# Retiming the attention tasks of the first layer and splitting weight panels in halves

## The chip, the cores and the metric

The kernel runs on one core of one Trainium2 chip. Its time is the device time of one execution in microseconds (us), and the figure to compare is the median of several runs. PE is the matrix engine (TensorE), DVE the vector engine, ACT the scalar engine, POOL GpSimd, SP the engine that issues most DMAs. Each engine carries out its own instructions in order; semaphores tie them together.

## The reference

Four layers transform 256 latent tokens of width 1024. The two layers of the first block also carry 256 context tokens in the first of them. The change touches the mixer of layer 0, which adds two branches, and the treatment of the weights of all four layers.

```python
def mla_attend(q, k, v):            # branch 1: 8 heads, softmax attention
    s = einsum('bhqd,bhkd->bhqk', qblk, k) * scale
    p = softmax(s, axis=-1)
    return einsum('bhqk,bhkv->bhqv', p, v)
...
def gla_chunked(q, k, v, logg, s0): # branch 2: 4 heads, chunks of 64 tokens
    b = cumsum(logg.reshape(B, H, n, C, DK), axis=3)
    q_dec, k_inv, k_end = q * exp(b), k * exp(-b), k * exp(b[..., -1:, :] - b)
    a = where(incl, einsum('bhnid,bhnjd->bhnij', q_dec, k_inv), 0.0)
    o_intra = einsum('bhnij,bhnjv->bhniv', a, v)
    def step(s, xs):
        o = einsum('bhcd,bhdv->bhcv', qd_c, s)
        s = s * ge_c[..., None] + einsum('bhcd,bhcv->bhdv', ke_c, v_c)
        return s, o
```

Latent queries attend to all 512 keys, context queries to the 256 context keys. The recurrence (`gla_chunked`) runs forwards and backwards. Its output is normalised, gated, joined to the attention output and multiplied by `even_w_out`.

## The kernel before

**Weights.** All weights are stored as 204 panels, nearly all 128 x 2048 f32. SP streams them into three slots `raw`. ACT copies a panel to a rounded 32-bit form `w_high` (`split_act`, L355), DVE subtracts to get the remainder `w_low` (`split_dve`, L361), and PE then multiplies three times: low x high, high x high, high x low (`product3`, L389 to L391). `w_high` and `w_low` have two buffers each, so the copy of panel m waits until PE is done with panel m-2. PE waits for a panel's `w_low` before its first product.

**Attention tasks of layer 0.** There are 32 tasks (query tile i of 0 to 3, head h), all heads of tile 0 first. Tiles 0 and 1 are latent: 512 keys, a long task. Tiles 2 and 3 are context: 256 keys, a short task. Each task passes these stations: PE scores (L1399), DVE row maximum (`maxima`, L1525), ACT exponential (`exps`, L1476), PE transposes of the probabilities (`turn`, L1407), ACT copy out (`probs_out`, L1483), PE product with the values (`values`, L1418). PE's loop body is

```python
turn(n); scores(n + 2); gla_step(n); values(n)
```

ACT's is `exps(n); probs_out(n-1); gla_step(n)`, DVE's `maxima(n); gla_step(n)`. After 8 tasks of a tile DVE scales their sum (`scale`, L1531 and L1533).

**The recurrence among them.** `gla_step(n)` places pieces of the second branch at fixed task numbers on each engine: PE turns the keys (L1144), computes two groups of scores for each direction (L1159), which DVE masks (`mask_scores`, L1168), two groups of state updates (L1179), which DVE chains in seven steps (`gla_states`, L1188 and L1191), then outputs (L1207 and L1213), which ACT copies out (`outputs_out`, L1220 and L1221), sums of squares (L1228), roots on ACT (`roots`, L1233 and L1235, each with a table load) and gating on DVE (`gated`, L1240 and L1242). The gates of the backward direction are made in the first tasks (L1089 to L1138).

**Its end.** PE transposes the attention output (L1466), ACT and DVE split the eight blocks of features into high and low (L1516, L1519, L1566), and the product `even_out` starts (`linear`), taking blocks in the order that it is given.

Of the kernel before, what the change touches and what calls it, by code (L numbers as in the profile page):

```python
# [8 lines left out]
F32 = mybir.dt.float32  # L9
# [8 lines left out]
P = 128  # L18
# [268 lines left out]
class Program:  # L287
# [61 lines left out]
    def split_act(self, act, m, q=None):  # L349
        slot, width = m % RAW, PLAN[m]  # L350
        act.wait_ge(self.landed[slot], self.in_loop(self.landed_count, m, q))
        if m - 2 >= self.layer_m:
            sem = self.ends[m - 2][0]
            act.wait_ge(sem, self.in_loop(lambda x: self.ends[x][1], m - 2, q))
        self.nc.scalar.activation(self.wh[:, m % 2, 0:width], self.raw[:, slot, 0:width],  # L355
                                  ACT.Copy).then_inc(self.w_high, 1)

    def split_dve(self, dve, m, q=None):
        slot, width = m % RAW, PLAN[m]
        dve.wait_ge(self.w_high, self.in_loop(lambda x: x + 1, m, q))  # L360
        self.nc.vector.tensor_tensor(self.wl[:, m % 2, 0:width], self.raw[:, slot, 0:width],  # L361
                                     self.wh[:, m % 2, 0:width].bitcast(F32),
                                     ALU.subtract).then_inc(self.w_split, 1)

    def split_upto(self, which, eng, m):
        while self.split_next[which] <= m:
# [11 lines left out]
            self.split_upto("dve", dve, self.m + count - 1)  # L378

    def wait_split(self, pe, m, q=None):  # L380
        pe.wait_ge(self.w_split, self.in_loop(lambda x: x + 1, m, q))

    def product3(self, out, sh, sl, mh, ml, nk, opens=True, closes=True):

# [10 lines left out]
    def stream(self, end):  # L395

        total = min(end + RAW, len(PLAN))

        @self.block.sync
        def _(sp):  # L400
            n = self.streamed
            while n < RAW:
                sp.dma_start(self.raw[:, n, :], self.panels[n, :, :]).then_inc(self.landed[n], 16)
                n += 1
            turns = (total - n) // RAW
            with sp.Fori(0, turns) as q:
                for s in range(n, n + RAW):
                    sp.wait_ge(self.w_split, q * RAW + (s - RAW + 1))
                    sp.dma_start(self.raw[:, s % RAW, :],
                                 self.panels[ds(q * RAW + s, 1), :, :].rearrange("a p n -> p (a n)")  # L410
                                 ).then_inc(self.landed[s % RAW], 16)
            for n in range(n + turns * RAW, total):
                sp.wait_ge(self.w_split, n - RAW + 1)
# [604 lines left out]
def even_mixer(pr, mod, scope, norm_w, x_ready, beside, rest):  # L1018
# [346 lines left out]
    def beside_uv(which, eng, p):  # L1365
        if which == "dve":
# [27 lines left out]
    def _(pe):  # L1394
# [16 lines left out]
        def values(n):  # L1411
            i, h = tasks[n]
            keys = width(n) // P
            pe.wait_ge(t_out, n + 1)
            if h == 0 and i >= 2:
                pe.wait_ge(a_scaled, i - 1)
            for j in range(keys):
                last = nc.tensor.matmul(ps[:, 4 + i % 2, h * MV:(h + 1) * MV], prob_t[:, n % 2, j * P:(j + 1) * P],  # L1418
                                        v[:, first_key(i) // P + j, h * MV:(h + 1) * MV],
                                        start=(j == 0), stop=(j == keys - 1))  # L1420
            last.then_inc(v_done, 1)

        def gla_step(n):
            if n == 2:
# [4 lines left out]
            if n in (7, 8):  # L1429
                gla_updates(pe, 0, n - 7)  # L1430
            if n == 9:
                pe.wait_ge(s_ready[0], 2)
                turn_keys(pe, 1)
            if n in (10, 11):
                gla_scores(pe, 1, n - 10)
            if n in (13, 14):
                gla_updates(pe, 1, n - 13)
            if n in (16, 17):
                gla_outputs(pe, 0, (0, 1) if n == 16 else (2, 3))
            if n in (19, 20):  # L1440
                gla_outputs(pe, 1, (0, 1) if n == 19 else (2, 3))
            if n in (22, 24):
                square_sums(pe, (n - 22) // 2)

        pe.wait_ge(z_taken[0], 1)
        gate_products(pe, 1)
# [13 lines left out]
        for i in range(4):  # L1460
            pe.wait_ge(a_scaled, i + 1)
            if i == 0:
                pe.wait_ge(p_ready, T)
                pe.wait_ge(t_out, T)
            for b in range(4):
                last = nc.tensor.transpose(ps[:, b, i * P:(i + 1) * P], att[:, i, b * P:(b + 1) * P], c("ident"))  # L1466
                if i == 3:
                    last.then_inc(a_turned, 1)

    @pr.block.scalar  # L1470
    def _(act):
# [12 lines left out]
                .then_inc(t_out, 1)  # L1484

        def gla_step(n):
            if n == 1:
                gate_abs(act, 1)
            if n == 2:
                gate_log(act, 1)  # L1490
            if n == 3:
                keys_out(act, 0)
            if n == 4:
                decays_first(act, 1)
            if n == 5:
                decays_second(act, 1)
            if n == 10:
                keys_out(act, 1)
            if n in (18, 21):
                outputs_out(act, (n - 18) // 3)  # L1500
            if n in (22, 24):
                act.wait_ge(o_done, 2)
                pr.split_upto("act", act, pr.m + (n - 22) // 2)
            if n in (23, 25):
                roots(act, (n - 23) // 2)

        for n in range(T + 1):
            if n < T:
# [2 lines left out]
                probs_out(n - 1)  # L1511
            gla_step(n)
        act.wait_ge(s_done, T)
        for k in range(4):
            act.wait_ge(o_gated, k // 2 + 1)
            nc.scalar.activation(high[:, 4 + k, :], gla[:, k, :], ACT.Copy).then_inc(y_high, 1)  # L1516
        for b in range(4):
            act.wait_ge(a_turned, b + 1)
            nc.scalar.activation(high[:, b, :], ps[:, b, :], ACT.Copy).then_inc(y_high, 1)  # L1519

    @pr.block.vector
    def _(dve):
# [3 lines left out]
                .then_inc(m_ready, 1)  # L1526

        def scale(i):
            group = slice(i * H, (i + 1) * H)
            dve.wait_ge(p_ready, (i + 1) * H)  # L1530
            ch.then(dve, nc.vector.reciprocal(inv[:, group], total[:, group]))  # L1531
            dve.wait_ge(v_done, (i + 1) * H)
            nc.vector.tensor_tensor(att[:, i, :].rearrange("p (h n) -> p h n", n=MV),  # L1533
                                    ps[:, 4 + i % 2, :].rearrange("p (h n) -> p h n", n=MV),
                                    spread(inv[:, group], 2, MV), ALU.mult).then_inc(a_scaled, 1)

        def gla_step(n):
            if n == 1:
                gate_min(dve, 1)
            if n == 3:  # L1540
                gate_sums(dve, 1)
            if n in (4, 5):
                mask_scores(dve, 0, n - 4)
            if n == 6:
                decayed(dve, 1)
            if n in (7, 8):
                gla_states(dve, 0, n - 7)
            if n in (10, 11):
                mask_scores(dve, 1, n - 10)
            if n in (13, 14):  # L1550
                gla_states(dve, 1, n - 13)
            if n in (23, 25):
                pr.split_upto("dve", dve, pr.m + (n - 23) // 2)
            if n in (24, 26):
                gated(dve, (n - 24) // 2)

        for n in range(T):
            maxima(n)
            gla_step(n)
            if n >= H and (n - 1) % H == 0:  # L1560
                scale(n // H - 1)
        scale(3)
        for k in range(8):
            dve.wait_ge(y_high, k + 1)
            src = gla[:, k, :] if k < 4 else ps[:, k - 4, :]
            nc.vector.tensor_tensor(low[:, (k + 4) % 8, :], src, high[:, (k + 4) % 8, :].bitcast(F32),  # L1566
                                    ALU.subtract).then_inc(y_split, 1)

    return high, low, [(y_split, KD)], later

# [1260 lines left out]
def build(nc, panels, rows, conditions, small, xin, pos, out):  # L2831
    with ExitStack() as ctx:
# [41 lines left out]
        def layer0():  # L2874
# [6 lines left out]
            def _(sp):  # L2881
# [17 lines left out]
            ready = pr.linear("even_out", 4, 2, 8, pr.features(high, low, TA, KD, tall_offset, [4, 5, 6, 7, 0, 1, 2, 3]),  # L2899
                              pr.add_gated(mod, 16, 2, TA), y_split, engines=("dve",), banks=(4, 5, 6, 7),  # L2900
                              after=gates_ready, rising=True,
                              beside=lambda which, eng, p: take_rest(eng, 2) if which == "dve" else None)
# [120 lines left out]
```

## Time and profile before

| | |
|---|---|
| median of 3 runs | 2465.21 us (2463.22 to 2465.62) |
| profiled execution | 2460.01 us, span 2458.2 us |
| PE busy | 2077.2 us (85%), mean granted clock 0.920 |
| DVE busy | 1528.6 us (62%) |
| ACT busy | 869.9 us (35%) |
| attention stage, first scores to the first product of `even_out` | 221.44 to 393.83 us |

Busy time counts compute instructions; the granted clock is a share of TensorE's full speed. In the rows below a time in front is the start within the span, the next the duration; "x8" is that many instructions merged; a bracket says how long the engine was idle before and what ended that. The trace counts every 32-bit matmul of L1159, L1179, L1399 and L1418 as two instructions. In the tables of windows a stretch is followed by the busy time of each engine and by the granted clock under PEclk.

### The profile page before, as it was taken

The numbers are of one execution on the slowest core, as the hardware profiler recorded it, in microseconds if no ns is written. First come the engines' busy times: TensorE is split into PE (matmuls) and PEld (weight loads), VectorE is DVE, ScalarE is ACT, GpSimd is POOL, SyncE is SP. The second block draws the span as 40 slices with busy tenths as digits, with TensorE's granted clock in tenths as the row PEclk, the third lists the DMA queues.
The fourth block names the chain that finished last, engine by engine and source line by source line (L and its number), as shares of the span: only waits on it lengthen the run. The fifth ranks groups of instructions, "written<-read, shape, count | busy, mean of one in ns | idle before, by whom it ended". The sixth has DMA issues, their size and how long they took to land. (4 is left out here: it accounts for less than half of the span.)

```text
span 2458.2 us, 39406 instructions
## 1 busy us (share of the span) xinstructions
PE 2077.2 (85%) x16738; PEld 1843.5 (75%) x16738; DVE 1528.6 (62%) x2187; ACT 869.9 (35%) x1104; POOL 140.3 (6%) x231
## 2 busy tenths in 40 slices
PE   0898679799999588769996999699789979978997
PEld 0686467577888476568886899688679978867997
DVE  7865326699777556655654666668466656845444
ACT  2335233322222222142224444345443334534442
POOL 0000000000110001010210000000000000000000
PEclk9999688899999779879998999889899988979999
DMA  7432002355553245300001477433147733313552
GB/s 303 153 136 69 1 16 88 111 176 179 201 192 140 99 159 184 119 2 3 3 3 56 169 262 265 173 120 123 67 145 267 266 144 137 121 52 105 186 188 86
DMA packets 59018, 323.89 MB, mean 132 GB/s; under 512 B 6272, under 2 KB 7424, under 8 KB 32512
## 3 DMA queue, kind: packets, MB, share of 16 engines
q1 hardware_dynamic: 32960, 227.91, 26.1%
q0 software_dynamic: 25344, 92.29, 10.6%
q8 instruction: 105, 1.72, 0.3%
q10 hardware_dynamic: 576, 1.70, 0.2%
q14 instruction: 33, 0.27, 0.0%
HBM read 320.83 MB, written 1.05 MB: 131 GB/s over the span
## 5 line engine op out<-in xcount | busy, mean ns | idle before, releaser
L361 DVE TENSOR_TENSOR w_low<-raw,w_high 128x2048 fp32r<-128x2048 f32 (+1 forms) x204 | 458.9, 2252 | 323.6 <-ACT w_high L355 323.4
L355 ACT ACTIVATE w_high<-raw 128x2048 fp32r<-128x2048 f32 (+1 forms) x204 | 382.8, 1878 | 427.9 <-PE banks L391 382.2
L498 DVE SCALAR_TENSOR_TENSOR mod_rows<-mod_rows,silu_condition 128x1024 f32<-128x1024 f32 x176 | 212.4, 1221 | 48.2 <-DMA mod_rows<-rows_dram 46.6
L389 PE MATMUL banks<-ffn_a_l,w_high 128*128 128x256 f32 x704 | 201.0, 285 | 5.5 <-DVE ffn_hidden L860 5.5
L390 PE MATMUL banks<-ffn_a_h,w_high 128*128 128x256 f32 x704 | 199.4, 283 | 0.0
L391 PE MATMUL banks<-ffn_a_h,w_low 128*128 128x256 f32 x704 | 199.3, 283 | 0.0
L389 PE MATMUL banks<-mlp_a_l,w_high 128*128 128x512 f32 (+1 forms) x512 | 177.9, 347 | 17.8 <-DVE mlp_hidden L862 10.0
L484 POOL DMA_DIRECT2D mod_rows<-rows_dram x176 | 93.1, 529 | 1542.8 <-DVE mod_rows L498 1389.2
L389 PE MATMUL banks<-mlp_hidden_l,w_high 128*128 128x512 f32 (+1 forms) x512 | 173.7, 339 | 3.1 <-DVE mlp_hidden_l L868 2.1
L391 PE MATMUL banks<-mlp_a_h,w_low 128*128 128x512 f32 (+1 forms) x512 | 175.2, 342 | 0.0
L390 PE MATMUL banks<-mlp_a_h,w_high 128*128 128x512 f32 (+1 forms) x512 | 175.2, 342 | 0.0
L390 PE MATMUL banks<-mlp_hidden_h,w_high 128*128 128x512 f32 (+1 forms) x512 | 173.0, 338 | 0.0
L391 PE MATMUL banks<-mlp_hidden_h,w_low 128*128 128x512 f32 (+1 forms) x512 | 173.0, 338 | 0.0
L389 PEld LDWEIGHTS banks<-ffn_a_l,w_high 128*128 128x128 f32 x704 | 133.9, 190 | 10.7 <-issue 5.9
L389 PE MATMUL banks<-mix_l,w_high 128*128 128x256 f32 x432 | 127.6, 295 | 11.8 <-DVE mix_l L631 7.9
L390 PEld LDWEIGHTS banks<-ffn_a_h,w_high 128*128 128x128 f32 x704 | 133.9, 190 | 0.0
L391 PEld LDWEIGHTS banks<-ffn_a_h,w_low 128*128 128x128 f32 x704 | 133.8, 190 | 0.0
L389 PEld LDWEIGHTS banks<-mlp_a_l,w_high 128*128 128x128 f32 x512 | 97.9, 191 | 36.8 <-issue 14.4
L390 PE MATMUL banks<-mix_h,w_high 128*128 128x256 f32 x432 | 123.8, 287 | 0.0
L391 PE MATMUL banks<-mix_h,w_low 128*128 128x256 f32 x432 | 123.5, 286 | 0.0
L389 PEld LDWEIGHTS banks<-mlp_hidden_l,w_high 128*128 128x128 f32 x512 | 96.4, 188 | 16.4 <-DVE mlp_y L880 3.2
L391 PEld LDWEIGHTS banks<-mlp_a_h,w_low 128*128 128x128 f32 x512 | 97.9, 191 | 11.7
(582 smaller groups left out, 4930.9 us busy)
## 6 DMA issues: line engine op xcount, KB each, us to landing
raw<-panels_dram SPq DMA_DIRECT2D x204, 1024.0 KB, 4.8
mod_rows<-rows_dram POOLq DMA_DIRECT2D x176, 512.0 KB, 5.0
mod_0a_rows<-rows_dram SPq DMA_DIRECT2D x4, 2048.0 KB, 24.9
x_features<-x_features_dram SPq DMA_DIRECT2D x1, 2048.0 KB, 25.2
constants<-small_dram SPq DMA_DIRECT2D x1, 1660.5 KB, 16.3
silu_condition<-conditions_dram ACTq DMA_DIRECT2D x3, 512.0 KB, 5.9
out_dram<-x_features SPq DMA_DIRECT2D x1, 1024.0 KB, 4.8
constants<-small_dram SPq DMA_DIRECT2D x1, 736.5 KB, 5.5
```

The source lines that it names most:

```text
L355: self.nc.scalar.activation(self.wh[:, m % 2, 0:width], self.raw[:, slot, 0:width], ACT.Copy).then_inc(self.w_high, 1)
L361: self.nc.vector.tensor_tensor(self.wl[:, m % 2, 0:width], self.raw[:, slot, 0:width], self.wh[:, m % 2, 0:width].bitcast(F32), ALU.subtra ...
L389: self.nc.tensor.matmul(out, sh(k), ml(k), start=(opens and k == 0), stop=False)
L390: self.nc.tensor.matmul(out, sh(k), mh(k), start=False, stop=False)
L391: last = self.nc.tensor.matmul(out, sl(k), mh(k), start=False, stop=(closes and k == nk - 1))
L484: pool.dma_start(buffers[i % nb], self.rows[at, :, :]).then_inc(landed[i % nb], 16)
L498: nc.vector.scalar_tensor_tensor(row if v == nv - 1 else self.scratch[:], row, 1.0, self.cond[v][:], ALU.mult, ALU.mult, accum_out=mod[:, ...
```

## The change

1. Every panel is split in two halves by columns: two ACT copies, two DVE subtractions, each DVE half waiting for its ACT half; PE still waits for both.
2. Tasks of a long and a short tile alternate (tiles 0 and 2, then 1 and 3), and PE issues `turn(n+1)` and `scores(n+3)` ahead of `gla_step(n)` and `values(n)`.
3. The pieces of the recurrence sit at other task numbers; DVE and ACT take what PE made for them two or three task numbers later than before.
4. `scale` and the final splitting follow the new order; `gated` moves from inside the loop to behind it, and `even_out` takes blocks in the order 4, 5, 0, 1, 2, 3, 6, 7.

```diff
-        self.nc.scalar.activation(self.wh[:, m % 2, 0:width], self.raw[:, slot, 0:width],
-                                  ACT.Copy).then_inc(self.w_high, 1)
+        for h in range(2):
+            cols = slice(h * width // 2, (h + 1) * width // 2)
+            self.nc.scalar.activation(self.wh[:, m % 2, cols], self.raw[:, slot, cols],
+                                      ACT.Copy).then_inc(self.w_high, 1)
...
+        for h in range(2):
+            cols = slice(h * width // 2, (h + 1) * width // 2)
+            dve.wait_ge(self.w_high, self.in_loop(lambda x: 2 * x + h + 1, m, q))
+            self.nc.vector.tensor_tensor(self.wl[:, m % 2, cols], ...).then_inc(self.w_split, 1)
...
-    tasks = [(i, h) for i in range(4) for h in range(H)]
+    tasks = [(i, h) for first in range(2) for h in range(H) for i in (first, first + 2)]
...
+        turn(0)
+        scores(2)
         for n in range(T):
-            turn(n)
-            if n + 2 < T:
-                scores(n + 2)
+            if n + 1 < T:
+                turn(n + 1)
+            if n + 3 < T:
+                scores(n + 3)
             gla_step(n)
             values(n)
...
-            if n in (4, 5):                       # PE
-                gla_scores(pe, 0, n - 4)
+            if n in (3, 5):
+                gla_scores(pe, 0, (n - 3) // 2)
...
-            if n in (4, 5):                       # DVE
-                mask_scores(dve, 0, n - 4)
+            if n in (6, 8):
+                mask_scores(dve, 0, (n - 6) // 2)
...
-            if n in (22, 24):                     # ACT
+            if n in (28, 30):
                 act.wait_ge(o_done, 2)
-                pr.split_upto("act", act, pr.m + (n - 22) // 2)
+                pr.split_upto("act", act, pr.m + (n - 28) // 2)
-            if n in (23, 25):
-                roots(act, (n - 23) // 2)
+            if n in (29, 31):
+                roots(act, (n - 29) // 2)
...
-        scale(3)
+        gated(dve, 0)
+        scale(1)
+        scale(3)
+        gated(dve, 1)
```

On PE, around the first scores of the recurrence (L1159, in the changed file L1163), before the change; L1407 are the turned probabilities, L1399 the scores, L1418 the values:

```order
L1407 MATMUL banks<-constants,even_pa 128x128 x4
L1399 MATMUL banks<-mla_k,mla_q 128x512
L1159 MATMUL banks<-even_y 128x128 x8
L1418 MATMUL banks<-mla_v,mla_prob_t 128x64 x4
L1407 MATMUL banks<-constants,even_pa 128x128 x4
L1399 MATMUL banks<-mla_k,mla_q 128x512
L1159 MATMUL banks<-even_y 128x128 x8
```

The same place on PE in the changed kernel, where these three lines are L1411, L1403 and L1422:

```order
L1411 MATMUL banks<-constants,even_pa 128x128 x4
L1403 MATMUL banks<-mla_k,mla_q 128x512
L1163 MATMUL banks<-even_y 128x128 x8
L1422 MATMUL banks<-mla_v,mla_prob_t 128x64 x2
L1411 MATMUL banks<-constants,even_pa 128x128 x2
L1403 MATMUL banks<-mla_k,mla_q 128x256
L1422 MATMUL banks<-mla_v,mla_prob_t 128x64 x4
L1411 MATMUL banks<-constants,even_pa 128x128 x4
L1403 MATMUL banks<-mla_k,mla_q 128x512
L1163 MATMUL banks<-even_y 128x128 x8
```

The two groups of scores now have a task without a piece between them, and a row of L1411 turns the task after the one whose values follow it.

On DVE the maxima (L1525) and the masking (L1168) of the forward direction before the change:

```order
L1525 TENSOR_REDUCE mla_stat<-banks 128x1
L1168 COPY_PREDICATED gla_att<-constants,banks 128x1024
L1525 TENSOR_REDUCE mla_stat<-banks 128x1
L1168 COPY_PREDICATED gla_att<-constants,banks 128x1024
L1525 TENSOR_REDUCE mla_stat<-banks 128x1
```

The same place on DVE in the changed kernel (L1533 and L1172), with the three products of `decayed` (L1139 to L1142) now in between:

```order
L1533 TENSOR_REDUCE mla_stat<-banks 128x1 x3
L1172 COPY_PREDICATED gla_att<-constants,banks 128x1024
L1533 TENSOR_REDUCE mla_stat<-banks 128x1
L1139 TENSOR_TENSOR gla_work_230<-even_pb,gla_work_230 128x1024
L1140 SCALAR_TENSOR_TENSOR gla_work_231<-even_pb,gla_work_231 128x1024
L1142 TENSOR_TENSOR gla_work_231<-even_pb,gla_work_231 128x1024
L1533 TENSOR_REDUCE mla_stat<-banks 128x1
L1172 COPY_PREDICATED gla_att<-constants,banks 128x1024
```

Three maxima stand ahead of the first masking where one stood, so the maxima of the tasks whose scores PE has issued are out before DVE waits for the recurrence.

On ACT the last tasks of the changed kernel (L1483 exponential, L1490 copy out, L357 panel halves, L1237 and L1239 roots):

```order
L357 ACTIVATE w_high<-raw 128x1024 x2
L1483 ACTIVATE even_pa,mla_stat<-banks,mla_stat 128x256
L1490 ACTIVATE mla_prob_t<-banks 128x512
L1237 ACT_TABLE_LOAD
L1237 ACTIVATE even_y<-banks,constants 128x1024
L1239 ACT_TABLE_LOAD
L1239 ACTIVATE even_y<-even_y 128x1024
L1490 ACTIVATE mla_prob_t<-banks 128x256
L1524 ACTIVATE even_h<-even_pa 128x512 x2
```

The second root now stands directly ahead of the last task's copy out; before, six tasks stood between them.

## Rows read from the trace of the kernel before

**Rows 1.** Windows: the attention stage, and two stretches of it.

```profile
221.40:394.00 172.60, 123.28 (x746) 95.17 (x746) 56.71 (x92) 64.17 (x128) 2.80 (x4) 0.75 0.06 19
326.60:337.00 10.40, 10.39 (x55) 9.37 (x56) 1.65 (x4) 2.52 (x8) 0.00 (x0) 0.56 0.01 2
337.00:361.00 24.00, 20.96 (x192) 18.56 (x190) 2.12 (x5) 7.76 (x18) 0.00 (x0) 0.93 0.00 1
```

**Rows 2.** Waits in the attention stage: engine, line, releaser, total us, times, longest.

```profile
PE banks L1418 <- ACT mla_prob_t L1483: 48.6, 17, 4.6
```

**Rows 3.** Timeline of one long task with its recurrence piece.

```profile
286.36 1.88 PE L1144 MATMUL banks<-constants,gla_work 128*128 128x128 f32 x8
288.07 1.01 PE L1418 MATMUL banks<-mla_v,mla_prob_t 128*128 128x64 f32 x8
...
290.31 1.16 PE L1159 MATMUL banks<-gla_work 64*128 64x128 f32 x16
291.59 1.29 DVE L1168 COPY_PREDICATED gla_att<-constants,banks 128x1024 f32<-128x1024 uint32 x1 [9.48 <-PE banks L1159]
...
293.49 0.69 ACT L1476 ACTIVATE even_pa<-banks,mla_stat 128x512 f32<-128x512 f32 x1 [4.19 <-DVE mla_stat L1525]
...
294.80 1.91 PE L1418 MATMUL banks<-mla_v,mla_prob_t 128*128 128x64 f32 x8 [3.33 <-ACT mla_prob_t L1483]
```

**Rows 4.** Timeline of PE: half of an output piece, a short task, sums of squares.

```profile
354.05 1.08 PEld L1207 LDWEIGHTS banks<-gla_att,even_gv 128*128 128x128 f32 x8
...
357.96 0.66 PE L1418 MATMUL banks<-mla_v,mla_prob_t 128*128 128x64 f32 x4
...
360.80 0.66 PE L1418 MATMUL banks<-mla_v,mla_prob_t 128*128 128x64 f32 x4 [1.52 <-ACT mla_prob_t L1483]
...
361.95 1.88 PE L1228 MATMUL banks<-even_y,constants 128*128 128x512 f32 x4
```

**Rows 5.** Timeline: one group of state updates at full clock.

```profile
265.33 1.10 PE L1179 MATMUL banks<-even_gv,even_y 64*64 64x128 f32 x28
```

**Rows 6.** Timeline of DVE: the gate sums' start, and the maximum behind them.

```profile
233.37 1.23 DVE L1109 TENSOR_TENSOR gla_work<-gla_work,gla_work 128x1024 f32<-128x1024 f32 x1 [4.12 <-ACT gla_work L1104]
...
239.40 0.68 DVE L1525 TENSOR_REDUCE mla_stat<-banks 128x1 f32<-128x512 f32 x1
```

**Rows 7.** Timeline of ACT: an output copied out, and one root with table loads.

```profile
344.45 1.02 ACT L1221 ACTIVATE even_y<-banks 128x1024 f32<-128x1024 f32 x1
...
363.29 1.28 ACT L1233 ACT_TABLE_LOAD   x1
...
367.97 0.46 ACT L1476 ACTIVATE even_pa<-banks,mla_stat 128x256 f32<-128x256 f32 x1
```

**Rows 8.** Timeline of the stage's end: last copy out, first product of `even_out`.

```profile
389.59 0.38 ACT L1483 ACTIVATE mla_prob_t<-banks 128x256 f32<-128x256 f32 x1 [0.97 <-PE banks L1407]
...
393.83 0.50 PE L389 MATMUL banks<-even_l,w_high 128*128 128x512 f32 x1
```

**Rows 9.** The page's costliest groups: busy, mean ns, idle before and releaser.

```profile
L361 DVE TENSOR_TENSOR w_low<-raw,w_high 128x2048 fp32r<-128x2048 f32 (+1 forms) x204 | 458.9, 2252 | 323.6 <-ACT w_high L355 323.4
L355 ACT ACTIVATE w_high<-raw 128x2048 fp32r<-128x2048 f32 (+1 forms) x204 | 382.8, 1878 | 427.9 <-PE banks L391 382.2
```

**Rows 10.** Waits of PE in the whole kernel behind panels and hidden activations.

```profile
PE banks L389 <- DVE w_low L361: 11.0, 6, 3.0
PE banks L389 <- DVE mlp_hidden L862: 10.0, 16, 2.5
...
PE banks L389 <- DVE ffn_hidden L860: 5.5, 11, 0.9
```

**Rows 11.** Timeline of a feed-forward turn in layer 1: panel, modulation row, hidden activation.

```profile
1475.22 2.29 DVE L361 TENSOR_TENSOR w_low<-raw,w_high 128x2048 fp32r<-128x2048 f32 x1 [1.98 <-ACT w_high L355]
...
1478.57 0.69 DVE L862 SCALAR_TENSOR_TENSOR mlp_hidden<-banks,mlp_activated 128x512 f32<-128x512 f32 x1
```

**Rows 12.** Timeline: DVE operations of 1024 columns, back to back.

```profile
205.16 1.22 DVE L1136 SCALAR_TENSOR_TENSOR even_y<-even_pb,even_y 128x1024 f32<-128x1024 f32 x1
206.30 1.22 DVE L1138 TENSOR_TENSOR even_y<-even_pb,even_y 128x1024 f32<-128x1024 f32 x1
```

More of the change, by code:

```diff
@@ L1414, in values @@
             pe.wait_ge(t_out, n + 1)
-            if h == 0 and i >= 2:
-                pe.wait_ge(a_scaled, i - 1)
+            if h == 0 and i % 2:
+                pe.wait_ge(a_scaled, i // 2 + 1)
             for j in range(keys):
-                last = nc.tensor.matmul(ps[:, 4 + i % 2, h * MV:(h + 1) * MV], prob_t[:, n % 2, j * P:(j + 1) * P],
+                last = nc.tensor.matmul(ps[:, 4 + i // 2, h * MV:(h + 1) * MV], prob_t[:, n % 2, j * P:(j + 1) * P],
                                         v[:, first_key(i) // P + j, h * MV:(h + 1) * MV],
@@ L1453, in _ @@
         scores(1)
+        turn(0)
+        scores(2)
         for n in range(T):
-            turn(n)
-            if n + 2 < T:
-                scores(n + 2)
+            if n + 1 < T:
+                turn(n + 1)
+            if n + 3 < T:
+                scores(n + 3)
             gla_step(n)
             values(n)
-        for i in range(4):
-            pe.wait_ge(a_scaled, i + 1)
+        for n, i in enumerate((0, 2, 1, 3)):
+            pe.wait_ge(a_scaled, n + 1)
             if i == 0:
@@ L1513, in _ @@
         act.wait_ge(s_done, T)
[L1514 to L1519, printed above, removed]
+        for k in (4, 5, 0, 1, 2, 3, 6, 7):
+            if k >= 4:
+                act.wait_ge(o_gated, k // 2 - 1)
+                nc.scalar.activation(high[:, k, :], gla[:, k - 4, :], ACT.Copy).then_inc(y_high, 1)
+            else:
+                act.wait_ge(a_turned, k + 1)
+                nc.scalar.activation(high[:, k, :], ps[:, k, :], ACT.Copy).then_inc(y_high, 1)
     @pr.block.vector
@@ L1541, in gla_step @@
                 gate_sums(dve, 1)
-            if n in (4, 5):
-                mask_scores(dve, 0, n - 4)
-            if n == 6:
+            if n in (6, 8):
+                mask_scores(dve, 0, (n - 6) // 2)
+            if n == 7:
                 decayed(dve, 1)
[L1546 to L1555, printed above, removed]
+            if n in (10, 12):
+                gla_states(dve, 0, (n - 10) // 2)
+            if n in (16, 18):
+                mask_scores(dve, 1, (n - 16) // 2)
+            if n in (20, 22):
+                gla_states(dve, 1, (n - 20) // 2)
+            if n in (29, 31):
+                pr.split_upto("dve", dve, pr.m + (n - 29) // 2)
         for n in range(T):
@@ L1559, in _ @@
             gla_step(n)
-            if n >= H and (n - 1) % H == 0:
-                scale(n // H - 1)
-        scale(3)
[L1563 to L1567, printed above, removed]
+            if n == 17:
+                scale(0)
+            if n == 18:
+                scale(2)
+        gated(dve, 0)
+        scale(1)
+        scale(3)
+        gated(dve, 1)
+        for n, k in enumerate((4, 5, 0, 1, 2, 3, 6, 7)):
+            dve.wait_ge(y_high, n + 1)
+            nc.vector.tensor_tensor(low[:, k, :], gla[:, k - 4, :] if k >= 4 else ps[:, k, :],
+                                    high[:, k, :].bitcast(F32), ALU.subtract).then_inc(y_split, 1)
     return high, low, [(y_split, KD)], later
@@ L2898, in layer0 @@
                 pr, mod, ab, norm("norm1", 0), mod_ready + [(x_in, 16)], beside, rows_rest)
-            ready = pr.linear("even_out", 4, 2, 8, pr.features(high, low, TA, KD, tall_offset, [4, 5, 6, 7, 0, 1, 2, 3]),
+            ready = pr.linear("even_out", 4, 2, 8, pr.features(high, low, TA, KD, tall_offset, [4, 5, 0, 1, 2, 3, 6, 7]),
                               pr.add_gated(mod, 16, 2, TA), y_split, engines=("dve",), banks=(4, 5, 6, 7),
```

64 lines of the change are left out of this document (32 added, 32 removed).

## The prediction

> **What bounds the kernel now.** I read the page first, then the windows by stage, the waits, and the timeline of the stage that the change rewrites. The windows show the attention stage of layer 0 taking 172.6 us, with PE busy 123.28 us at a mean granted clock of 0.75 [rows 1]. The waits name the cause: PE stood 48.6 us in 17 places ahead of the values L1418 until ACT had copied out the probabilities [rows 2]. The timeline shows why. PE issues scores of the recurrence L1159 at 290.31; DVE takes them at 291.59, having waited 9.48 us in its own order; only then come the maximum and at 293.49 ACT's exponential of the next task, and ACT's order has the copy out of this task behind that exponential; so the values of this task wait 3.33 us, to 294.80 [rows 3]. Four maskings and four chains of states repeat this circle. It has a second price: the same eight instructions of L1418 took 1.01 us at 288.07 and 1.91 us at 294.80 [rows 3]. The second runs after PE stood still, at half the clock.
>
> In the rest of the kernel PE is mostly the bound. Each weight panel goes ACT 1878 ns, then DVE 2252 ns, and DVE stood 323.4 us in total waiting for ACT in this [rows 9]. That matters only where PE waits behind it.
>
> **The attention stage, part by part.** The new order breaks the circle. PE issues `scores(n+3)`, so the maximum of task n+2 or n+3 is out before DVE waits for the recurrence piece of task n. ACT copies task n's probabilities out while PE turns n+1. So I add up what PE itself must do, at full clock, from the starts of following rows. A long task: values at 288.07 to the piece at 290.31, 2.24 us [rows 3]. A short one: 360.80 to 361.95, 1.15 us [rows 4]. Sixteen of each: 54.2 us. Recurrence: turned keys 286.36 to 288.07 at half clock, so 0.86, twice, 1.7; scores 1.16 x 4 = 4.6 [rows 3]; updates 1.10 x 4 = 4.4 [rows 5]; output halves 354.05 to 357.96, 3.91 x 4 = 15.6; squares 1.88 x 2 = 3.8 [rows 4]. In all 84.3 us, where the stage before took 393.83 - 221.44 = 172.4 us.
>
> PE isn't the bound to the end. ACT's last pieces hang on the last output half. Behind that half PE has only the squares (3.8) and the rest of five tasks (about 4.6 tasks of 1.7, 7.9 us), so it ends 84.3 - 11.7 = 72.6 us of PE work in. ACT then has, in its order: copying the output out, two of 1.02, 2.0 us [rows 7]; two panels of 1.88, 3.8 us [rows 9]; two roots with two table loads each, 363.29 to 367.97, 4.68 x 2 = 9.4 us [rows 7]; and exponentials and copies of four and a half tasks at about 1 us each (the exponential alone is 0.69 at 293.49 [rows 3]), 4.5 us. Together 19.7 us, more than PE's 11.7. The last copy out, which now stands behind the second root, comes there. From it to `even_out` there were 393.83 - 389.59 = 4.2 us [rows 8]. The changed DVE order puts `gated(1)`, two operations of 1.22 us [rows 12], ahead of the splitting of the first block: 0 to 2.4 us more, I take 1.2, since fewer transposes are left by then. 5.4 us.
>
> Stalls that stay: at the start the first exponential must come before the first turn, 1.4 us; ACT's log of the backward gates has the pattern of a root, 4.7 us [rows 7], and the third exponential now stands behind it, 4.5 us; the gate sums hold DVE from 233.37 to the maximum at 239.40, 6 us [rows 6], of which about 1.5 us stick out over the slack of two tasks; the three products of `decayed`, 3 x 1.22 us [rows 12] ahead of a maximum, 2 us. Together 9.4 us.
>
> Sum at full clock: 72.6 + 19.7 + 5.4 + 9.4 = 107.1 us. Two allowances. After each of these early stalls the clock falls, as in [rows 3], and work of about 10 us runs at half: 10 us. Handovers that the sum passes over, a few tenths in some places of thirty: 6 us. The stage comes to about 124 us, **48 us less**. Bounds: neither allowance, 107, 65 less; all PE work up to the last output half at half clock, below.
>
> **The clock** is the weak point. PE was busy 10.39 of 10.40 us from 326.6 on and had only 0.56 of full clock; from 337 to 361, in the same mixture, it had 0.93 with 20.96 of 24 us busy [rows 1]. So continuous work takes a while to be granted full clock, and keeps it over short gaps. The Trainium skill, "TensorE: Matmul & The Clock Gate", Part 1, says that the throttled clock is the default and activity releases it, and under HAM oscillation that a kernel with repeated idle gaps starts each burst cold. By that rule a stage whose stalls go gets the full clock for nearly all its work, the upper bound of the gain; the slow first row above says that the trace agrees only with delay.
>
> **The halves.** Per panel one more ACT and one more DVE instruction. DVE: two of 1.22 us against 2.25, at most 0.19 more [rows 9, 12]; back to back they start 1.14 us apart (205.16, 206.30), so at least 0.03 [rows 12]. ACT: two of 1.02 (a copy of 1024 columns [rows 7]) against 1.88, at most 0.16. Panel to ready goes from 1.88 + 2.25 = 4.13 us to 1.02 + 2.3 = 3.3: 0.8 us sooner wherever DVE stands waiting. The feed-forward turn shows it: DVE waited 1.98 us for ACT, subtracted for 2.29 us, made a modulation row, and came to the hidden activation at 1478.57, for which PE then waited [rows 11]. Those PE waits are 10.0 us in 16 places and 5.5 us in 11, and 6 on panels themselves, 11.0 us [rows 10]. Mean waits of 0.5 to 0.6 us lie below the 0.8 us gained, so about 12 us of the 15.5 go, and 6 x 0.8 = 4.8 of the 11.0: 17 us. Against that, DVE or ACT lie on the path between products, at norms and in the mixers, where up to a fifth of the 204 panels may be: 40 x 0.13 = 5 us. Net **12 us less**; bounds 17 less and, with 71 us (204 x 0.35) wholly on the path and no gain, 71 more.
>
> The Trainium skill, "VectorE: DVE Perf Modes", section on the TRN2 errata, says that VectorE and ScalarE pay a fixed extra per instruction on SBUF sources and asks for large tiles, which speaks against the halves. "Perfetto Trace Analysis", Optimizing Scalar/DVE Operations, puts about 60 ns (VectorE) and 93 ns (ScalarE) on each; by it 204 panels cost 31 us of engine time, an estimate from that page, little of it on the path. [Rows 12] agree with a small fixed cost. It also allows breaking up instructions where they leave bubbles on other engines.
>
> **Sum.** 2460.0 (profiled execution) - 48 - 12 = 2400. That execution lay 5.2 us under the median, so against the median 2465.2 - 60 = **2405 us**. What a measurement of this kernel can tell from no change is about 0.2%, 5 us.
>
> **Rivals.**
> - *Everything overlaps and the clock stays full* (chance 0.12). 65 less in the stage, 17 in the halves: 2465 - 82 = 2383. For it: [rows 1] from 337 on. Against it: the early stalls are in the order itself.
> - *Stalls move instead of going* (0.17). DVE's chains of states or ACT's wait for an output hold the next maximum or exponential after all, because tasks are now only 1.7 us long on average, less than the 2.24 us of today's long ones, so two tasks of slack are 3.4 us. If half of the 48.6 us [rows 2] stays, the stage gains 24 us: 2465 - 24 - 12 = 2429.
> - *Half clock throughout* (0.09). If the stage never earns full clock, 72.6 us becomes 72.6 x 1.9 = 138 (1.91 against 1.01 us [rows 3]) and the stage 138 + 19.7 + 5.4 + 9.4 = 172.5, as before. Only the halves count: 2453. For it: the first window of [rows 1]; this is what the skill's rule makes of a loop whose matmuls stay too sparse.
> - *The change doesn't do what it says* (0.06). The tail on ACT or another order lengthens the stage by what the loop saves and the halves give about what they cost: 2455 to 2470.
> - *Slower* (0.04). The second half's instruction lies on the path of nearly every panel, because DVE's order, not PE, paces the layers: 204 x 0.35 = 71 us more, 48 less from attention: 2488. It decides from 0.24 us per panel (48/204) on. Against it: DVE waited for ACT at these panels for 323.4 us [rows 9], so it has time.
>
> **Numbers.** My forecast has 0.52, with a range of its own of 2390 to 2422. With the cases on both sides, 2387 to 2445 leaves out part of the first rival, the half clock and the slower cases. Faster by over 0.2%: 0.52 + 0.12 + 0.17 + 0.09 = 0.90; within 0.2%: 0.05; slower: 0.05.
>
> **What would show it.** The stage from the first scores to the first product of `even_out` should last 115 to 130 us, with a clock of 0.85 or more. PE's wait ahead of the values should fall from 48.6 to under 12 us. ACT should be busy nearly without gaps in the last 20 us, PE idle there. The waits of PE for `mlp_hidden` and `ffn_hidden` should fall from 15.5 to about 4 us. ACT's and DVE's halves should be near 1.0 and 1.2 us, 408 of each. I am wrong if the clock stays near 0.75 with PE busy throughout, if DVE's chains of states still end long waits of ACT's exponential, or if the layers after the first get longer.

## The result

The changed kernel takes 2366.82 us (median of 4 runs, 2366.02 to 2374.3), the kernel before 2464.22 us in the same comparison (4 runs). The ratio is 0.9614, 95% interval 0.9591 to 0.9638: 97 us less. The direction was forecast, the size wasn't: 2405 us with a range from 2387 was 38 us too slow, and even the rival in which everything goes well (2383 us) was.

The profiled execution has a span of 2365.3 us against 2458.2, so 92.9 us less. The time between the same two places in each kernel:

| stretch | before, us | after, us | less |
|---|---|---|---|
| first scores to first product of `even_out` | 172.4 | 107.8 | 64.6 |
| feed-forward of layer 0, first to last hidden activation | 330.2 | 327.7 | 2.5 |
| feed-forward of layer 1, the same | 181.5 | 171.1 | 10.3 |
| feed-forward of layer 2, the same | 176.4 | 169.7 | 6.8 |
| feed-forward of layer 3, the same | 170.5 | 169.7 | 0.8 |
| all the rest (mixers, norms) | | | 7.9 |

**The attention stage.** The windows of the changed kernel, first the whole stage, then a part near its start, its middle and its end; the columns are those of [rows 1]:

```profile
221.37:329.14 107.77, 93.47 (x745) 73.87 (x745) 55.52 (x92) 63.94 (x130) 2.76 (x4) 0.92 0.09 30
231.60:238.00 6.40, 6.40 (x35) 5.18 (x36) 5.02 (x6) 3.57 (x10) 0.00 (x0) 0.73 0.01 3
238.00:305.00 67.00, 65.45 (x611) 53.18 (x611) 31.76 (x62) 30.92 (x77) 0.00 (x0) 0.97 0.01 1
305.00:329.14 24.14, 16.82 (x80) 12.60 (x79) 13.36 (x17) 21.08 (x32) 0.00 (x0) 0.79 0.25 87
```

From 238 to 305 us PE is busy 65.45 of 67 us at a granted clock of 0.97. The whole stage has 0.92 where [rows 1] had 0.75. PE's two largest sums of waits in it:

```profile
PE banks L1411 <- ACT even_pa L1483: 11.0, 5, 4.2
PE banks L1422 <- ACT mla_prob_t L1490: 2.2, 1, 2.2
```

The 48.6 us ahead of the values of [rows 2] are down to 2.2. In their place stand 11.0 us ahead of the turn, three at the start (1.16, 4.18 and 1.55 us) and two at the end (0.62 and 3.45 us). The timeline shows the first masking of the recurrence, the piece that held everything up in [rows 3]; L1163 is PE's piece, L1422 the values, L1411 the next turn:

```profile
238.88 1.16 PE L1163 MATMUL banks<-even_y 64*128 64x128 f32 x16
...
239.97 0.66 PE L1422 MATMUL banks<-mla_v,mla_prob_t 128*128 128x64 f32 x4
240.16 1.31 DVE L1172 COPY_PREDICATED gla_att<-constants,banks 128x1024 f32<-128x1024 uint32 x1 [0.48 <-PE banks L1163]
...
240.47 0.39 PE L1411 MATMUL banks<-constants,even_pa 128*128 128x128 f32 x2
```

PE goes from its piece to the values and on to the next turn without a bracket, that is without having been idle, and DVE masks beside it. The start and the tail:

```profile
231.59 0.95 PE L1411 MATMUL banks<-constants,even_pa 128*128 128x128 f32 x4 [4.18 <-ACT even_pa L1483]
...
304.43 1.02 ACT L1224 ACTIVATE even_pa<-banks 128x1024 f32<-128x1024 f32 x1 [3.88 <-PE banks L1217]
...
323.61 0.36 ACT L1490 ACTIVATE mla_prob_t<-banks 128x256 f32<-128x256 f32 x1
...
329.14 0.47 PE L393 MATMUL banks<-even_l,w_high 128*128 128x512 f32 x1 [1.10 <-DVE even_l L1577]
```

**The halves.** The page's groups of the changed kernel, to be set against [rows 9]:

```profile
L365 DVE TENSOR_TENSOR w_low<-raw,w_high 128x1024 fp32r<-128x1024 f32 (+1 forms) x408 | 472.8, 1201 | 268.4 <-ACT w_high L357 268.1
L357 ACT ACTIVATE w_high<-raw 128x1024 fp32r<-128x1024 f32 (+1 forms) x408 | 401.8, 1034 | 434.0 <-PE banks L395 388.5
```

DVE's busy time rose by 13.9 us, 68 ns for each of 204 added instructions, ACT's by 19.0 us, 93 ns each. The Trainium skill, "Perfetto Trace Analysis", Optimizing Scalar/DVE Operations, gives about 60 and 93 ns; ACT's figure here is the same, DVE's is 8 ns higher.

PE's waits behind panels and hidden activations in the whole kernel, where [rows 10] had 11.0, 10.0 and 5.5 us:

```profile
PE banks L393 <- DVE w_low L365: 9.3, 5, 3.2
...
PE banks L393 <- DVE mlp_hidden L866: 4.0, 2, 2.5
...
PE banks L393 <- DVE ffn_hidden L864: 1.9, 2, 0.9
```

Two successive hidden activations of layer 1's feed-forward in the changed kernel:

```profile
1402.96 0.69 DVE L866 SCALAR_TENSOR_TENSOR mlp_hidden<-banks,mlp_activated 128x512 f32<-128x512 f32 x1
...
1414.35 0.69 DVE L866 SCALAR_TENSOR_TENSOR mlp_hidden<-banks,mlp_activated 128x512 f32<-128x512 f32 x1
```

and the one that followed the row at 1478.57 of [rows 11] in the kernel before:

```profile
1490.62 0.69 DVE L862 SCALAR_TENSOR_TENSOR mlp_hidden<-banks,mlp_activated 128x512 f32<-128x512 f32 x1
```

A turn took 12.05 us and takes 11.39. This is what PE did before the change at the wait behind that row at 1478.57:

```profile
1478.53 0.28 PE L390 MATMUL banks<-mlp_hidden_h,w_high 128*128 128x256 f32 x1
1478.64 0.28 PE L391 MATMUL banks<-mlp_hidden_h,w_low 128*128 128x256 f32 x1
1479.31 0.39 PE L389 MATMUL banks<-mlp_a_l,w_high 128*128 128x256 f32 x1 [0.39 <-DVE mlp_hidden L862]
1479.53 0.29 PE L390 MATMUL banks<-mlp_a_h,w_high 128*128 128x256 f32 x1
```

In an unbroken row the products start 0.12 us apart. Here 0.67 us pass from one start to the next and then 0.22, so the row loses 0.65 us, though the bracket counts 0.39 of idle: it counts from the modelled end of the last product, 1478.92, and in an unbroken row each product overlaps the next. The lost 0.65 us are nearly the whole 0.66 by which the turn shrank.

### The profile page after: what moved, and what is told of

It is laid out like the page before. It is cut to its first block and busy times, and to the rows that moved or that the text cites. A ratio compares the mean times of both kernels' runs of the same rounds, so it can differ in the third digit from the quotient of the medians.

```text
span 2365.3 us, 39903 instructions
## 1 busy us (share of the span) xinstructions
PE 2036.8 (86%) x16738; PEld 1818.3 (77%) x16738; DVE 1540.9 (65%) x2391; ACT 888.1 (38%) x1308; POOL 140.3 (6%) x231
## 5 line engine op out<-in xcount | busy, mean ns | idle before, releaser
L365 DVE TENSOR_TENSOR w_low<-raw,w_high 128x1024 fp32r<-128x1024 f32 (+1 forms) x408 | 472.8, 1201 | 268.4 <-ACT w_high L357 268.1
L357 ACT ACTIVATE w_high<-raw 128x1024 fp32r<-128x1024 f32 (+1 forms) x408 | 401.8, 1034 | 434.0 <-PE banks L395 388.5
L394 PEld LDWEIGHTS banks<-mlp_a_h,w_high 128*128 128x128 f32 x512 | 98.0, 192 | 10.9
## 6 DMA issues: line engine op xcount, KB each, us to landing
constants<-small_dram SPq DMA_DIRECT2D x1, 1660.5 KB, 16.3
```

The costliest lines, as they stand in the source:

```text
L357: self.nc.scalar.activation(self.wh[:, m % 2, cols], self.raw[:, slot, cols], ACT.Copy).then_inc(self.w_high, 1)
L365: self.nc.vector.tensor_tensor(self.wl[:, m % 2, cols], self.raw[:, slot, cols], self.wh[:, m % 2, cols].bitcast(F32), ALU.subtract).then_ ...
L394: self.nc.tensor.matmul(out, sh(k), mh(k), start=False, stop=False)
```

## The experiments

Ratios are to runs of the kernel before on the same chip. "Stage" is the stretch in the first line of the table above.

**1. The halves alone.** The kernel before with the edits to `split_act`, `split_dve`, `wait_split` and `stream`, nothing else.

```diff
+        for h in range(2):
+            cols = slice(h * width // 2, (h + 1) * width // 2)
...
+            dve.wait_ge(self.w_high, self.in_loop(lambda x: 2 * x + h + 1, m, q))
```

> The kernel before with the panel halves alone. Theory A (the two parts are independent; the layers behind layer 0 shrank by 28 us through the halves alone): attention stage 172 us as before, whole kernel about 2436 us, feed-forward turns 11.4 us in layer 1 and 17.1 us in layer 2 (12.06 and 17.7 before). Rival B (the later layers gained from an earlier start of modulation rows and DMA, not from the halves): the turns keep 12.06 and 17.7 us and the kernel stays at 2455 to 2470 us.

Measured 2434.48 us against 2461.18, ratio 0.988 (0.9859 to 0.99): 26.7 us less. The stage doesn't shrink: it has 176.8 us in the profiled execution, 4.4 more than before, at the same mean clock of 0.75. That execution was the slowest of the four, 7.6 us above their median, so whether the halves lengthen this stage is not shown. The feed-forward stretches are those of the changed kernel within 1.4 us: 329.0, 171.1, 169.7 and 169.7 us. PE's waits for hidden activations are too:

```profile
PE banks L393 <- DVE mlp_hidden L866: 4.0, 2, 2.5
PE banks L393 <- DVE ffn_hidden L864: 1.9, 2, 0.9
```

Theory A holds, rival B falls: the later layers gain through the halves, whatever attention does.

**2. The attention order alone.** The changed kernel with whole panels.

```diff
-        for h in range(2):
-            cols = slice(h * width // 2, (h + 1) * width // 2)
+        self.nc.scalar.activation(self.wh[:, m % 2, 0:width], self.raw[:, slot, 0:width], ...)
```

> The changed kernel with whole panels. Theory A: attention stage about 108 us with its clock at 0.92, the rest as before, whole kernel about 2400 us. Rival B: about 2370 us, since the later layers shrink here too. Rival C (the halves also shorten the tail of the stage by letting DVE start sooner): stage 112 us or more.

Measured 2394.5 us, ratio 0.9724 (0.9704 to 0.9743): 66.7 us less. The window of the stage:

```profile
220.89:327.27 106.38, 92.28 (x746) 73.48 (x745) 55.32 (x90) 63.56 (x128) 2.77 (x4) 0.92 0.09 31
```

106.4 us, 1.4 us less than with halves, so rival C falls, and rival B with it. The two gains add up: 26.7 + 66.7 = 93.4 of 97.4 us, and 0.988 x 0.9724 = 0.9607 beside the measured 0.9614.

**3. Without alternation.** Run-ahead, late taking and halves kept, the tasks tile by tile.

```diff
-    tasks = [(i, h) for first in range(2) for h in range(H) for i in (first, first + 2)]
+    tasks = [(i, h) for i in range(4) for h in range(H)]
...
+            if n in (10, 18, 26):
+                scale((n - 10) // 8)
```

> The changed kernel with the tasks in their old order, all heads of a tile before the next tile: run-ahead, later taking and halves stay. Long tasks come first, all short ones last, beside the output pieces and ACT's roots. Theory A (alternation is a minor part: the PE work is the same sum): stage 108 to 114 us, whole kernel 2367 to 2373 us. Rival D (alternation carries the gain, because short tasks alone are shorter than ACT's and DVE's pieces, and four of them don't cover a root): stage above 120 us, kernel above 2380 us.

Measured 2368.88 us, ratio 0.9616 (0.9597 to 0.9636). The window of the stage:

```profile
220.47:328.94 108.47, 92.86 (x745) 73.85 (x745) 55.70 (x92) 63.42 (x130) 2.76 (x4) 0.92 0.09 30
```

108.5 against 107.8 us. Rival D falls. With run-ahead and late taking in place, alternating long and short tasks brings nothing here that can be measured; without them it was not tried.

**4. Without run-ahead.** PE's old loop body with the new task numbers.

```diff
-        turn(0)
-        scores(2)
         for n in range(T):
-            if n + 1 < T:
-                turn(n + 1)
-            if n + 3 < T:
-                scores(n + 3)
+            turn(n)
+            if n + 2 < T:
+                scores(n + 2)
...
-                eng.wait_ge(o_out, 1)
+                eng.wait_ge(o_squared, 1)
```

> The changed kernel with PE's old loop body (turn n, scores n+2, piece, values n); the later taking, alternation and halves stay; the second output piece also waits for the squares of the first. Theory E (the later taking breaks the circle, run-ahead only hides ACT's copy out): the waits ahead of the values come back at every task for the copy out, 0.5 to 1 us in 32 places, stage 125 to 140 us, kernel about 2390 us. Rival F (without run-ahead the values of task n wait for the exponential of n+1, which waits for DVE just as before): stage near 165 us, kernel about 2430 us.

Measured 2383.85 us, ratio 0.9685 (0.9663 to 0.9706). Window and longest waits of PE in the stage:

```profile
220.93:341.98 121.05, 96.64 (x745) 73.67 (x745) 54.94 (x92) 64.36 (x131) 2.77 (x4) 0.92 0.08 27
...
PE banks L1422 <- ACT mla_prob_t L1487: 10.3, 5, 3.7
PE banks L1183 <- DVE gla_att L1172: 2.8, 2, 2.4
PE banks L1211 <- DVE gla_work L1195: 1.8, 1, 1.8
```

Rival F falls. The stage has 121.1 us, below theory E's 125 to 140: ahead of the values there are 10.3 us in 5 places, not a wait at each of 32. New are waits of PE for DVE's results of the recurrence. So run-ahead is worth 13 us of the 64.6 by the stage in the profiled executions, and 17 us by the medians of the whole kernel.

**5. Taken early.** Run-ahead stays, but DVE takes PE's pieces one task number behind PE instead of three.

```diff
-            if n in (6, 8):
-                mask_scores(dve, 0, (n - 6) // 2)
+            if n in (4, 6):
+                mask_scores(dve, 0, (n - 4) // 2)
...
-            if n in (10, 12):
-                gla_states(dve, 0, (n - 10) // 2)
+            if n in (8, 10):
+                gla_states(dve, 0, (n - 8) // 2)
```

> The changed kernel, but DVE masks the scores and chains the states one task number behind PE's piece instead of three (run-ahead, alternation, ACT's places and halves stay). Theory E (taking later is what breaks the circle): DVE waits for PE's piece with a maximum behind it that PE soon needs, eight times 1 to 3 us, stage 120 to 130 us, kernel 2380 to 2390 us, clock in the stage below 0.9. Rival G (run-ahead alone gives enough slack): stage 108 to 112 us, kernel within 5 us of the changed one (2367).

Measured 2405.72 us, ratio 0.9769 (0.9748 to 0.979). Window, PE's waits, and one chain of states in the timeline (L1183 PE's updates, L1192 and L1195 DVE's chain, L1483 the exponential):

```profile
220.91:359.64 138.73, 103.34 (x745) 80.85 (x745) 54.81 (x92) 62.59 (x130) 2.76 (x4) 0.87 0.07 24
...
PE banks L1411 <- ACT even_pa L1483: 28.4, 13, 4.2
...
256.04 1.98 PE L1183 MATMUL banks<-even_gv,even_y 64*64 64x128 f32 x28
...
258.06 0.29 DVE L1192 COPY even_y<-banks 128x128 f32<-128x128 f32 x1 [5.64 <-PE banks L1183]
258.39 2.27 DVE L1195 SCALAR_TENSOR_TENSOR even_y<-even_y,gla_g_end,banks 128x128 f32<-128x128 f32 x6
...
261.02 0.47 ACT L1483 ACTIVATE even_pa<-banks,mla_stat 128x256 f32<-128x256 f32 x1 [7.51 <-DVE mla_stat L1533]
...
261.64 0.63 PE L1411 MATMUL banks<-constants,even_pa 128*128 128x128 f32 x2 [2.86 <-ACT even_pa L1483]
```

DVE stood 5.64 us at the chain with the next maximum behind it, ACT waited 7.51 us for that maximum, PE 2.86 us for the exponential. Rival G falls. Theory E was right about the mechanism but not about the size: it forecast 120 to 130 us for the stage, which has 138.7, and 2380 to 2390 for the kernel, which has 2405.7. Late taking is worth 31 us by the stage, more than run-ahead. The profiled execution was 7 us faster than the median; by the medians of the whole kernel it is 39 us. Updates at half clock (1.98 us here, 1.10 in [rows 5]) are part of that.

**6. Rows later, whole panels.** The new attention order and whole panels. In the feed-forwards of layers 1 to 3 DVE makes its modulation rows behind the hidden activation (layer 3 has none to make).

```diff
                 split(which, m_of["down", cs, 0], q)(eng)
-                rows(eng, 1)
+                if not keep:
+                    rows(eng, 1)
                 if keep:
                     split(which, m_of["down", cs, 0] + 1, q)(eng)
-                    rows(eng, 2)
...
                 high_or_low(eng, cs + 1, q)
+                if keep:
+                    rows(eng, 1)
+                    rows(eng, 2)
```

> New attention order, whole panels, and in the feed-forwards with kept sums DVE makes its modulation rows behind the hidden activation's low part instead of ahead of the hidden activation. Theory H (PE waited because panel, subtraction and row stand ahead of the hidden activation in DVE's order; anything that takes 0.7 us out of that sum gives back 0.7 us a turn): turns of 11.4 us in layer 1 and 17.1 us in layer 2 as with the halves, kernel about 2383 us (17 of the halves' 28 us). Rival I (the halves gain by making panels ready for PE sooner, not through the hidden activation): turns stay at 12.06 and 17.7 us, kernel about 2400 us.

Measured 2378.36 us, ratio 0.9654 (0.9634 to 0.9675), 16 us less than experiment 2. Rival I falls. DVE in two successive turns of layer 1:

```profile
1408.48 0.68 DVE L862 SCALAR_TENSOR_TENSOR mlp_hidden<-banks,mlp_activated 128x512 f32<-128x512 f32 x1
...
1410.47 1.22 DVE L498 SCALAR_TENSOR_TENSOR mod_rows<-mod_rows,silu_condition 128x1024 f32<-128x1024 f32 x1
...
1419.88 0.68 DVE L862 SCALAR_TENSOR_TENSOR mlp_hidden<-banks,mlp_activated 128x512 f32<-128x512 f32 x1
```

The turn is 11.40 us with whole panels; that of layer 2 is 17.1 us. So the waits there came from the sum of what stood ahead of the hidden activation in DVE's order, and the halves are one way to shorten it. The fall of layer 1's stretch is 11.0 us and of layer 2's 6.0, within 1 us of the halves' 10.3 and 6.8.

**7. Quarters.**

```diff
-        for h in range(2):
-            cols = slice(h * width // 2, (h + 1) * width // 2)
+        for h in range(4):
+            cols = slice(h * width // 4, (h + 1) * width // 4)
```

> The changed kernel with panels in four quarters: 408 more instructions on ACT and on DVE. Theory H: a panel is ready at 0.55 + 4 x 0.6 = about 3.0 us instead of 3.4 us, but PE no longer waits in the feed-forward turns, so nothing is left to win there; the fixed cost (0.03 to 0.06 us per piece) is paid in the mixers and at norms: kernel 2366 to 2376 us. Rival J (readiness of panels still bounds the layers): 2355 to 2362 us.

Measured 2373.0 us, ratio 0.9635 (0.9615 to 0.9656), so rival J falls; 6 us above the changed kernel's 2366.8 and 4 above its repetition in experiment 9. The intervals of the ratios overlap, so a loss is not shown; there is no gain. The page:

```profile
L365 DVE TENSOR_TENSOR w_low<-raw,w_high 128x512 fp32r<-128x512 f32 (+1 forms) x816 | 500.5, 676 | 238.9 <-ACT w_high L357 236.9
L357 ACT ACTIVATE w_high<-raw 128x512 fp32r<-128x512 f32 (+1 forms) x816 | 440.0, 612 | 424.1 <-PE banks L395 377.0
```

408 more instructions each cost 27.7 us of DVE and 38.2 us of ACT, 68 and 94 ns apiece, as the first halving did. The feed-forward stretches of layers 1 to 3 hardly moved (170.7, 169.4 and 169.4 us).

**8. Joined roots.** ACT takes both roots in one go, with two table loads fewer, and both gatings come ahead of the last scaling.

```diff
-            if n in (29, 31):
-                roots(act, (n - 29) // 2)
+            if n == 29:
+                root_log(act, 0)
+                pr.split_upto("act", act, pr.m + 1)
+                root_log(act, 1)
+                root_exp(act, 0)
+                root_exp(act, 1)
```

> The changed kernel with ACT's two roots joined: logarithm 0, second panel, logarithm 1, then both exponentials, so two table loads fewer; both gatings ahead of the last scaling; blocks in the order 4, 5, 6, 7, 0, 1, 2, 3. Theory K (ACT's order bounds the last 23 us of the stage): two loads of 1.28 us and the 1.1 us wait of the first product go, stage 3 to 4.5 us shorter, kernel about 2363 us. Rival L (PE's order bounds the end): no change, 2367 us.

Measured 2368.73 us, ratio 0.9617 (0.9595 to 0.9638). Both expectations failed in part. The stage did shrink, to 105.9 us, and the last product of `even_out` started 2.1 us sooner (371.5 against 373.6 us), but nothing reached the end. Most of it is lost at the next norm, where PE sums squares. First the changed kernel, its timeline and a window:

```profile
376.66 7.13 PE L555 MATMUL banks<-norm_squares,constants 128*128 128x512 f32 x16 [2.67 <-ACT norm_squares L542]
...
376.00:383.00 7.00, 6.34 (x15) 2.96 (x16) 5.91 (x19) 5.53 (x10) 1.28 (x3) 1.00 0.93 355
```

Then the kernel with joined roots:

```profile
374.62 8.83 PE L555 MATMUL banks<-norm_squares,constants 128*128 128x512 f32 x16 [2.67 <-ACT norm_squares L542]
...
376.00:383.00 7.00, 7.00 (x15) 2.85 (x13) 3.90 (x15) 3.49 (x6) 0.00 (x0) 0.84 0.95 393
```

The same sixteen instructions, behind the same wait of 2.67 us, took 1.70 us longer at a clock of 0.84 instead of 1.00. It isn't the earlier arrival alone that does this: in experiment 3 the sixteen started at 376.49 and also took 8.83 us, in the kernel of experiment 10 they started at 375.96 and took 7.13. What decides it is not shown.

**9 to 11. The same, together.** The changed kernel once more, then it with the later rows, then it with later rows and joined roots, five rounds on one chip.

> The changed kernel itself, on the chip that runs the next two: about 2367 us, stage 108 us.

> The changed kernel, halves kept, with DVE's modulation rows of the kept feed-forwards behind the hidden activation. Theory H (halves and later rows remove the same wait of PE): nothing is left to gain in the turns, 11.4 and 17.0 us as in the changed kernel, kernel within 2 us of it. Rival I (they act in different places): the two gains of 28 and 16 us add up in part, kernel 2355 us or less.

> Halves, later rows and joined roots together. Stage about 106 us as with the joined roots. If the 1.9 us that these took off the stage carry to the end, 2364 to 2365 us; with theory H no more than that.

Measured 2369.31, 2369.62 and 2367.24 us, stages of 107.6, 107.6 and 105.8 us; ratios 0.9617 (0.9604 to 0.963), 0.9625 (0.9612 to 0.9638) and 0.9612 (0.9599 to 0.9625). Theory H holds: with the halves in place the later rows bring nothing (the turns are 11.4 and 17.1 us with and without them), so they remove the same wait. The combined version isn't measurably faster than the changed kernel.

## Why the prediction was wrong

**The circle, right.** Run-ahead and late taking broke it as described: the waits ahead of the values went from 48.6 to 2.2 us. Experiments 4 and 5 show that both are needed, at 13 and 31 us of the stage. The circle wasn't all of the 48.6 us, though. Eight of the 17 waits, four of 3.33 us and four of 4.6, stand behind a masking or a chain of states, 31.7 us together. The other nine stand at the start, behind output copies, behind ACT's roots (3.96 and 3.25 us) and in the last tasks. The changed kernel still has two waits behind the roots, 3.45 and 2.15 us. Some 20 of the 64.6 us belong to neither experiment alone: the wider spacing of PE's pieces and ACT's later places were never taken back by themselves.

**The step that failed in the stage: the two allowances.** The sum at full clock was 107.1 us, the stage took 107.8. To the sum I added 10 us for work at half clock and 6 us for handovers, 16 us where the stage shows under 4. (107.1 + 16 is 123.1; "about 124" is 0.9 too much.) The stalls at the start did lower the clock, to 0.73 from 231.6 to 238 us, but in 6.4 us that costs 1.7 us, and the 66.4 us at 0.97 behind it another 2.0: an estimate of 3.7 us from the windows, where I had 10. The last 24 us have a low clock (0.79), but up to 323.61 ACT paces them.

The parts of the sum came out close: the first output copy of the tail starts at 304.43, 83.1 us in, for 72.6 + 9.4 = 82.0 summed; from there to the last copy out 19.2 us, with ACT busy for 18.9 of them, for 19.7; from that to `even_out` 5.5, for 5.4. That the total agrees within 1 us is partly luck, since two errors in the first part cancel. The stalls were 6.9 us and not 9.4: the first exponential 1.16 for 1.4, ACT's logarithm 4.18 for 4.5, `decayed` 1.55 for 2, and the gate sums nothing for 1.5, because no wait of PE stands behind them. The rest was 76.2 us and not 72.6, which is what the low clock costs by the estimate; for handovers nothing is left over.

**The halves, right in kind, mis-sized.** Forecast were 12 us net with a bound of 17; alone they bring 26.7. Two terms failed. First, I took PE's recorded waits for hidden activations as all that was to be had, and about 12 us of the 15.5. The recorded waits fell by only 9.6 us, to 5.9, but the stretches of layers 1 and 2 shrank by 17.1 us, 0.69 and 0.68 a turn, where the wait recorded at a turn of layer 1 was mostly 0.38 to 0.54 us: the recorded idle of PE was not the whole delay, as its rows above show. The feed-forwards of layers 0 and 3 gave another 3.3. The waits behind panels, of which I expected 4.8 us back, fell by 1.7. Second, I set 5 us of cost for mixers and norms. What shows of it is about 1 us in the attention stage, 107.6 and 107.8 us in the two executions of the changed kernel, 106.4 and 106.8 in the two with whole panels (experiments 2 and 6).

What the halves do there is open. The table has 7.9 us less in the rest of the kernel, of which 4.1 lie between the feed-forwards of layers 2 and 3 (260.3 us before, 256.2 after). But that stretch also differs between executions of kernels that have the halves: 254.2 us in the changed kernel run again (clock 0.89), 260.4 in experiment 10 (clock 0.86). In experiment 1 the rest of the kernel was only 3.3 us shorter. So the gain in the feed-forwards is the halves' own, 20.4 us here and 19.0 in experiment 1, and the 7.9 us can't be counted as theirs. The price of the added instructions was right: 0.07 and 0.09 us, within the bounds of 0.03 to 0.19 and under 0.16.

**The 38 us.** The stage gave 64.6 us for 48, everything else 28.3 for 12: 16.6 and 16.3 us. Another 4.5 are that the medians lie 97.4 us apart and the profiled executions 92.9, and 1.0 that the kernel before had a median of 2464.2 us in this comparison instead of 2465.2.

**The rivals.** "Everything overlaps" was the nearest, and its bound of 65 us in the stage was met to half a microsecond. It missed by 16 us, 11 of them through its 17 us in the halves. "Half clock throughout" fell: [rows 1] showed PE busy at 0.56, but that stretch stood directly behind a series of stalls, which the new order doesn't have. "Stalls move" fell; experiment 5 is what it would have looked like. "The change doesn't do what it says" and "Slower" fell: both parts gain, the halves 26.7 us alone (experiment 1), the order 66.7 us alone (experiment 2). The Trainium skill's picture in "TensorE: Matmul & The Clock Gate", HAM oscillation, of throttling as what repeated idle gaps bring about, pointed to the upper bound of the gain, and the clock went from 0.75 to 0.92 as the gaps went.

## What to carry to other kernels

When a second chain of work is strewn into a pipelined loop, an in-order engine should take its results only after the loop's own instructions for the tasks that are already issued; here moving DVE's takers by two tasks was worth 31 us of the stage and PE's run-ahead 13, while mixing long and short tasks on top of them was worth nothing. Add up the bound engine's own work at full clock from starts of following rows, and size an allowance for slow clock by the length and the clock of the stretch behind a stall, not by a round number. PE's recorded idle in front of a product was less than the late operand cost here (0.39 against 0.65 us), so look at the time from turn to turn. Splitting the operand's preparation in two and moving unrelated work behind it removed the same wait, and four pieces brought nothing more.

## What was unexpected of the hardware

The same work behind the same wait was granted different clocks: sixteen matmuls of L555 after 2.67 us of idle took 7.13 us at a clock of 1.00 in one kernel and 8.83 us at 0.84 in another that came to this place 2 us sooner; of a gain of 2.1 us, 1.7 vanished in this. Of the nine profiled executions with halves five had 7.13 us here and four 8.83, and the slow one of experiment 3 came no sooner than the fast ones. Between the feed-forwards of layers 2 and 3 the same instructions on PE took from 254.2 to 260.4 us at clocks from 0.89 to 0.86. So a difference of a few microseconds in one stretch of one execution says little about a change.
